# Down projection of a gated feed-forward block in seven quarter products instead of eight

## Reference: what is computed

```python
def conv_glu_ffn(h, w_up, conv_w, w_down):
    u = causal_depthwise_conv(h @ w_up, conv_w)      # w_up 1024 x 5632, three taps
    gate, val = jnp.split(u, 2, axis=-1)
    return (jax.nn.silu(gate) * val) @ w_down        # w_down 2816 x 1024

for layer in range(DEPTH):
    ...
    x = x + rms_norm(m, mix_post_norm[layer])
    f = conv_glu_ffn(rms_norm(x, ffn_pre_norm[layer]), ffn_w_up[layer], ffn_conv_w[layer], ffn_w_down[layer])
    x = x + rms_norm(f, ffn_post_norm[layer])
```

## Time and profile before

| | us |
|---|---|
| median of 3 runs | 2688.99 |
| the profiled execution, its own time | 2685.92 |
| span of that execution (first to last instruction) | 2683.9 |
| TensorE busy (share) | 2599.2 (97%) |
| VectorE busy (share) | 1636.2 (61%) |
| ScalarE busy (share) | 1115.2 (42%) |
| GpSimd busy (share) | 1179.1 (44%) |
| mean granted TensorE clock | 0.991 |

### The profile page before, as it was taken

The page is one execution under the profiler, slowest core; times in us unless marked ns, Lnnn a source line. Parts: engine busy times, 40 slices in busy tenths (PEclk is TensorE's granted clock), DMA queues, the critical chain, the costliest instruction groups (busy, mean ns, idle before and its releaser), DMA issues. The chain is left out here.

```text
span 2683.9 us, 34327 instructions
## 1 busy us (share of the span) xinstructions
PE 2599.2 (97%) x12821; PEld 2156.9 (80%) x12821; DVE 1636.2 (61%) x1740; ACT 1115.2 (42%) x1645; POOL 1179.1 (44%) x721
## 2 busy tenths in 40 slices
PE   6999999999989999999999999999989999999998
PEld 5788888888778888888888688888878888888887
DVE  5677666676168666665455658557448666665454
ACT  6445545544443443433244334434533443433242
POOL 3444333434404778784443111111413877774442
PEclk9999999999999999999999999999999999999999
DMA  3111011111432222225554111012522222234553
GB/s 120 35 38 47 31 39 47 42 36 42 124 114 101 79 85 79 87 80 168 174 175 135 61 36 48 23 55 69 160 87 78 87 71 94 71 105 154 169 189 113
DMA packets 84541, 238.07 MB, mean 89 GB/s; under 512 B 8928, under 2 KB 22816, under 8 KB 84416
## 3 DMA queue, kind: packets, MB, share of 16 engines
q1 hardware_dynamic: 84416, 236.39, 26.6%
HBM read 189.66 MB, written 46.69 MB: 88 GB/s over the span
## 5 line engine op out<-in xcount | busy, mean ns | idle before, releaser
L391 POOL TENSOR_TENSOR f_wlo<-f_raw,f_whi 128x512 fp32r<-128x512 f32 (+1 forms) x210 | 426.5, 2032 | 499.4 <-ACT f_whi L432 499.4
L703 DVE TENSOR_TENSOR f_hlo<-f_hraw,f_hhi 128x512 fp32r<-128x512 f32 x88 | 182.1, 2075 | 200.9 <-ACT f_hhi L490 200.9
L432 ACT ACTIVATE f_whi<-f_raw 128x512 fp32r<-128x512 f32 (+1 forms) x210 | 171.9, 834 | 274.5 <-PE f_value L75 252.7
L391 POOL TENSOR_TENSOR f_wlo<-f_sums,f_whi 128x512 fp32r<-128x512 f32 x144 | 188.2, 1317 | 39.8 <-ACT f_whi L432 39.8
L432 ACT ACTIVATE f_whi<-f_sums 128x512 fp32r<-128x512 f32 x144 | 90.3, 627 | 270.7 <-POOL f_sums L397 270.7
L73 PE MATMUL f_value<-x_hi,f_whi 128*128 128x512 f32 x416 | 162.6, 391 | 1.6 <-POOL f_wlo L391 1.6
L74 PE MATMUL f_value<-x_lo,f_whi 128*128 128x512 f32 x416 | 162.6, 391 | 0.0
L75 PE MATMUL f_value<-x_hi,f_wlo 128*128 128x512 f32 x416 | 162.5, 391 | 0.0
L73 PE MATMUL f_part<-f_whi,f_hhi 128*128 128x512 f32 x352 | 137.9, 392 | 0.0
L75 PE MATMUL f_part<-f_whi,f_hlo 128*128 128x512 f32 x352 | 137.5, 391 | 0.0
L74 PE MATMUL f_part<-f_wlo,f_hhi 128*128 128x512 f32 x352 | 137.1, 389 | 0.0
(11 more groups left out here) (539 smaller groups left out, 7652.2 us busy)
## 6 DMA issues: line engine op xcount, KB each, us to landing
f_raw<-in_ffn_w_up SPq DMA_DIRECT2D x88, 512.0 KB, 3.6
f_raw<-in_ffn_w_down SPq DMA_DIRECT2D x88, 512.0 KB, 3.6
hidden<-f_hid SPq DMA_DIRECT2D x44, 512.0 KB, 2.8
f_hraw<-hidden SPq DMA_DIRECT2D x88, 256.0 KB, 3.9
g_raw_first<-in_gdn_w_in SPq DMA_DIRECT2D x16, 512.0 KB, 3.6
g_raw<-in_gdn_w_in SPq DMA_DIRECT2D x16, 512.0 KB, 4.2
f_xt<-x_mid SPq DMA_DIRECT2D x16, 512.0 KB, 4.8
l_raw_first<-in_gla_w_in SPq DMA_DIRECT2D x12, 512.0 KB, 3.6
```

Of the source, the lines that this page charges most:

```text
L391: pool.tensor_tensor(part_of(w_lo, k), source, part_of(w_hi, k).bitcast(F32), ALU.subtract) \
L432: act.activation(part_of(w_hi, k), source, ACT.Copy).then_inc(s_hi, 1)
L703: dve.tensor_tensor(h_lo[d % FFN_SLOTS][:, :], h_raw[d % HIDDEN_RAWS][:, :], plain32(h_hi[d % FFN_SLOTS][:, :]), ALU.subtract).then_inc(s_ ...
```

## The change

The down projection uses seven quarter products too. The hidden rows of pair 2k and 2k+1 and the halves of the 1024 output columns are taken as 2 by 2 blocks, so a product of 128x512 by 512 columns is needed for seven operand pairs in place of eight. There are 11 pairs k (`PAIRS`) and seven products, so 77 steps of 12 matmuls. Steps 0 to 21 are stage 0 (two products, plain rows), 22 to 43 stage 1 and 44 to 65 stage 2 (two products each, with weight sums), 66 to 76 stage 3 (the last product, tokens far).

- The sums of hidden rows (`hidden_sum`, four VectorE instructions of 128x512 for each k) are made in the up projection of the next even p, and stored to DRAM beside the rows: seven blocks of 256 KB for each k. `store_hidden` runs once for two p.
- GpSimd waits for the first k's fourth sum to be stored before it makes the first weight sums of the up projection. In the down projection it makes the low parts of the first eight steps only (`BY_POOL`); VectorE makes all the others (`down_low`), and the weight sums of stages 1 and 2 (`down_sums`: two and three instructions for each k).
- The products of stages 0 to 2 are joined on VectorE (`first_quarter`, `two_products`, `three_products`, `less_fourth`, `lead_row`, `last_row`), after ScalarE has copied the first product (`keep_products`).
- No norm runs before stage 3. The squares of `m_deviation` are written to `xn`, so it waits for the store of tile t-2; `x_deviation` writes them to the tile itself.
- Four steps are held, each of 12 matmuls, so three for each token tile and step. There are four buffers for hidden rows as loaded and four for their splits, in place of three and five.

```diff
-HIDDEN_RAWS = 3
+HIDDEN_RAWS = 4
+HIDDEN_SLOTS = 4
+PAIRS = FT // 2
+OPERANDS = 7
...
+    steps = [(stage, *step) for stage in range(3)
+             for step in ((0, 0), *(x for k in range(1, PAIRS) for x in ((0, k), (1, k - 1))), (1, PAIRS - 1))]
+    steps += [(3, 0, k) for k in range(PAIRS)]
+    STEPS = len(steps)
+    HELD = STEPS - HIDDEN_SLOTS
+    BY_POOL = 8
...
+    def tile_done(stage, second, i):
+
+        if i < NT // 2 - 1:
+            return s_part, 3 * (2 * stage + second) + i + 1
+        return s_prod, FIRST_DOWN + steps.index((stage, second, PAIRS - 1)) + 1
+
+    def h_raw(d):
+        return h_raw_in[0 if d < HIDDEN_RAWS or steps[d][0] == 3 else 1][d % HIDDEN_RAWS]
+
+    def down_source(d):
+        stage, second, k = steps[d]
+        e, o = rows_of(stage, k)
+        if stage in (1, 2):
+            return sums[:, 2 * (k % 2) + 1 - second, :]
+        if stage == 3:
+            return raw[o % FFN_RAWS][:, high_cols]
+        return raw[(o if second else e) % FFN_RAWS][:, low_cols]
+
+    def m_of(t):
+        return lead_rows[t] if t < NT // 2 else acc[t - NT // 2]
+
     block = ctx.enter_context(nc.Block())
...
+        def store_hidden(pair):
+            sp.wait_ge(s_h, 2 * pair + 2)
+            sp.dma_start(hidden[pair, 2:4].rearrange("o p t -> p o t"),
+                         hid[1][:, :].rearrange("p (o t) -> p o t", o=2)).then_inc(s_store[1], 16)
+            sp.wait_ge(s_hsum, 3 * pair + 1)
+            both = hidden_sums[min(pair, 1)]
+            sp.dma_start(hidden[pair, 4:6].rearrange("o p t -> p o t"), both).then_inc(s_sstore, 16)
+            sp.wait_ge(s_hsum, 3 * pair + 2)
+            sp.dma_start(hidden[pair, 0:2].rearrange("o p t -> p o t"),
+                         hid[0][:, :].rearrange("p (o t) -> p o t", o=2)).then_inc(s_store[0], 16)
+
+        def store_fourth(pair):
+            sp.wait_ge(s_hsum, 3 * pair + 3)
+            sp.dma_start(hidden[pair, 6], hidden_sums[min(pair, 1)][:, 0, :]).then_inc(s_fstore, 16)
 
...
             if d >= HIDDEN_RAWS:
                 sp.wait_ge(s_hlo, d - HIDDEN_RAWS + 1)
-            elif PLAIN < FT:
+                if d < 2 * HIDDEN_RAWS:
+                    sp.wait_ge(s_prod, FIRST_DOWN)
+            else:
                 sp.wait_ge(s_lo, FIRST_DOWN)
-            sp.dma_start(h_raw[d % HIDDEN_RAWS][:, :], hidden[k, :, near if d < FT else far]) \
...
+            if p and p % 2 == 0:
+                store_hidden(p // 2 - 1)
             load(2 * p + 6)
+            if p and p % 2 == 0:
+                store_fourth(p // 2 - 1)
             load(2 * p + 7)
             if p == FT - 2:
...
+            if d == HIDDEN_RAWS + 2:
+                store_hidden(PAIRS - 1)
+            if d == HIDDEN_RAWS + 6:
+                store_fourth(PAIRS - 1)
+            if 2 * FT + d + 2 < 2 * FT + 7 * PAIRS:
+                load(2 * FT + d + 2)
...
+            if d == 6 * PAIRS + HIDDEN_RAWS:
+                load_x(0)
+                load_x(1)
+        for t in range(NT):
+            if t == 1 and lead is not None:
+                sp.wait_ge(*low_done(STEPS - 1))
                 lead.load(sp)
...
+        pool.wait_ge(s_fstore, 16)
         for pair in range(PLAIN, FT):
             operands(pair)
-        for d in range(STEPS):
-            low(FIRST_DOWN + d, raw[(2 * FT + d) % FFN_RAWS][:, :])
+        for d in range(BY_POOL):
+            low(FIRST_DOWN + d, down_source(d))
         if lead is not None:
             lead.small_low(pool)
-            pool.wait_ge(s_lo, FIRST_DOWN + STEPS)
+            pool.wait_ge(*low_done(STEPS - 1))
...
+        def keep_products():
+            for i in range(NT // 2):
+                act.wait_ge(*tile_done(0, 0, i))
+                act.activation(lead_rows[i][:, low_cols], first_ps[i], ACT.Copy).then_inc(s_kept, 1)
 
         def m_deviation(t):
-            if t < NT // 2:
-                act.wait_ge(s_eva, t + 1)
-                act.wait_ge(s_evd, t + 1)
-                m = acc[t]
-            else:
-                act.wait_ge(s_m, t - NT // 2 + 1)
-                m = down_ps[t - NT // 2]
-            act.activation(squares[:, :], m[:, :], ACT.Square, accum_out=ss[:, t:t + 1])
+            act.wait_ge(s_mix, 16 + 2 * t + 2 if t < NT // 2 else 24 + t - NT // 2 + 1)
+            if t >= 2:
+                act.wait_ge(s_xout[t % 2], 16 * (t // 2))
+                if pre_gain is not None:
+                    act.wait_ge(s_xs, t - 1)
+            act.activation(xn[t % 2][:, :], m_of(t)[:, :], ACT.Square, accum_out=ss[:, t:t + 1])
...
+        for d in range(STEPS - HIDDEN_SLOTS):
+            down_high(d + 5)
+            high_hidden(d + HIDDEN_SLOTS)
+            if d + HIDDEN_SLOTS == steps.index((0, 0, PAIRS - 1)) + 3:
+                keep_products()
+            n = d + HIDDEN_SLOTS - 6 * PAIRS
+            if n == 3:
+                m_deviation(0)
+            elif n == 4:
+                m_deviation(1)
+            elif n == 6:
+                x_deviation(0)
+            elif n == 7:
+                m_deviation(2)
+            elif n == 8:
+                x_deviation(1)
+            elif n == 9:
+                x_high(0)
+        m_deviation(3)
+        x_high(1)
+        x_deviation(2)
         m_deviation(4)
         if lead is not None:
             lead.small_high(act)
+        x_high(2)
+        x_deviation(3)
+        m_deviation(5)
+        x_high(3)
+        if lead is not None:
+            act.wait_ge(*low_done(STEPS - 1))
+            lead.high(act)
         x_deviation(4)
-        x_high(0)
...
+        def hidden_sum(pair, n):
+
+            even, odd = hid[0], hid[1]
+            both = hidden_sums[min(pair, 1)]
+            dve.drain()
+            if n == 0:
+                if pair:
+                    dve.wait_ge(s_fstore, 16 * pair)
+                dve.tensor_tensor(both[:, 0, :], even[:, near], odd[:, near], ALU.add)
+            elif n == 1:
+                dve.tensor_tensor(both[:, 1, :], both[:, 0, :], even[:, far], ALU.subtract).then_inc(s_hsum, 1)
+                dve.tensor_tensor(even[:, near], even[:, far], even[:, near], ALU.subtract).then_inc(s_hsum, 1)
+            else:
+                dve.wait_ge(s_sstore, 16 * (pair + 1))
+                dve.tensor_tensor(both[:, 0, :], odd[:, far], both[:, 1, :], ALU.subtract).then_inc(s_hsum, 1)
+
+        def down_low(d):
...
+            if BY_POOL <= d < STEPS:
+                dve.wait_ge(s_hi, FIRST_DOWN + d + 1)
+                k = FIRST_DOWN + d
+                dve.tensor_tensor(part_of(w_lo, k), down_source(d), plain32(part_of(w_hi, k)), ALU.subtract) \
+                    .then_inc(s_dlo, 1)
...
+        def down_sums(d):
+
+            if d >= STEPS or steps[d][0] not in (1, 2) or steps[d][1]:
+                return
+            stage, _, k = steps[d]
+            rows = rows_of(stage, k)
+            e, o = (raw[n % FFN_RAWS] for n in rows)
+            first, second = (sums[:, 2 * (k % 2) + i, :] for i in range(2))
+            for n in rows:
+                dve.wait_ge(s_raw[n % FFN_RAWS], 16 * (n // FFN_RAWS) + 16)
+            dve.drain()
+            if stage == 1:
+                dve.tensor_tensor(first, e[:, high_cols], e[:, low_cols], ALU.subtract).then_inc(s_tsum, 1)
+                dve.drain()
+                dve.tensor_tensor(second, o[:, high_cols], first, ALU.subtract).then_inc(s_tsum, 1)
+                return
+            dve.tensor_tensor(first, o[:, high_cols], e[:, high_cols], ALU.subtract).then_inc(s_tsum, 1)
+            dve.drain()
+            dve.tensor_tensor(second, first, e[:, low_cols], ALU.add).then_inc(s_tsum, 1)
+            dve.drain()
+            dve.tensor_tensor(second, second, o[:, low_cols], ALU.subtract).then_inc(s_tsum, 1)
...
+        def first_quarter():
+            for i in range(NT // 2):
+                dve.wait_ge(s_kept, i + 1)
+                dve.wait_ge(*tile_done(0, 1, i))
+                quarter(acc[i][:, low_cols], second_ps[i], lead_rows[i][:, low_cols], ALU.add)
+
...
+        def lead_row(i):
+            dve.drain()
+            dve.wait_ge(*tile_done(2, 1, i))
+            x = lead_rows[i][:, low_cols]
+            quarter(lead_rows[i][:, high_cols], second_ps[i], acc[i][:, high_cols], ALU.add)
+            quarter(x, second_ps[i], x, ALU.add)
+
+        def last_row(i):
+            dve.drain()
+            dve.wait_ge(s_m, i + 1)
+            x = acc[i][:, high_cols]
+            quarter(x, first_ps[i], x, ALU.add)
...
+            if p == 1:
+                hidden_sum(0, 0)
+                hidden_sum(0, 1)
...
+        for d in range(6 * PAIRS):
+            if d - 1 in joins:
+                joins[d - 1]()
+            down_low(d + 4)
+            hidden_low(d + 3)
+            down_sums(d + 5)
+            if d == 1:
+                hidden_sum(PAIRS - 1, 0)
+                hidden_sum(PAIRS - 1, 1)
+            elif d == 4:
+                hidden_sum(PAIRS - 1, 2)
+        at = 6 * PAIRS + 3
```

(72 more changed lines are left out.)

321 lines of the change are left out of this document (156 added, 165 removed).

## The result

The changed kernel is slower. Four runs of it gave 2739.77 us as median (2737.35 to 2740.67), four of the kernel before on the same chip 2689.74; the ratio is 1.0186, with a 95% interval of 1.0169 to 1.0204. The forecast was 2669.5 us, so it missed by 70 us and had the wrong sign.

The account below looks back on a forecast made before the run. TensorE, busy 97% of the span, was taken to bound the kernel. Down projections -21.0 and -8.8 plus 2 x (1.5 + 3.0 + 0.7) gave -19.4 us, so 2669.5 us as median; range 2656 to 2698.

Parts of the forecast that it names:

- Up projection: Seven-product pairs: four more sums in every other pair fit VectorE's 13.7 us idle in two pairs, so cost nothing.
- My own sign of being wrong: Up projection: the prediction is wrong if seven-product pairs take over 19.1 us.
- Plain pairs: Up projection: a fourth sum ahead of the value convolution makes VectorE late; 0.7 us a layer (0 to 3).
- Start of the down projection: First steps of the down projection: waits of 2.0 and 1.0, together 3.0 us a layer (2 to 5).
- the first mechanism that I named: Down projection step 2: TensorE waits 2.0 us for `hidden_low(2)`, which stands behind `activated(21)`.
- The second mechanism: Down projection about step 7: rows and weights queue behind `store_hidden(10)`, which waits for the last sums; 1.0 us of wait.
- Stage 2: Down projection: splits wait for ScalarE's copy of summed weights, 5.6 us a k, mostly covered; 1.5 us a layer (0 to 4).
- Norms and tail: From step 66's start: 73.9 us to the mixer in the first layer, 49.0 to the end in the second.
- The slower one: Rival: VectorE and weight rows bound stages 1 and 2; at 7.4 us a k, 32 us lost, 2702; chance 0.15.
- The norm chain: Rival, behind step 66: a tile costs 1 us more or ScalarE's queue holds the last steps; 2685; chance 0.13.
- The clock: Rival, first layer's stage 3: idling TensorE runs at half clock, turns up to 5 us late; 2674; chance 0.10.
- The skill against it: `hidden_sum` in the first eight down-projection steps excludes GpSimd, costing the upper 6 us, 2 us more a layer: 2673.5.

Follow-up runs that it names:

- the exchange: Changed kernel with ScalarE's `keep_first` moved ahead of the high part of S3, the same instructions otherwise: 2687.35 us, ratio to the kernel before 0.9995.
- the new tail (last kernel): Changed kernel with `keep_first` and row splits earlier, norms interleaved behind step 66, squares of tiles 3 to 7 in `raw[0]`, last hidden sums later: 2655.29 us, ratio 0.987.
- the kernel before with four such instructions and the exchange: Kernel before plus four VectorE instructions of 128x512 per even pair on an unused tile, and `keep_first` ahead of S3's high part: 2686.87 us.

## Why the prediction was wrong, step by step

The forecast for the span was 2683.9 - 19.4 = 2664.5, and it came to 2738.6: 74.1 us. Of these the up projection is 46.8, the start of the down projections 13.4, stage 2 7.6, the part behind step 66 4.0, and unchanged code 2.8 (sum 74.6; in each layer 66 steps without a wait take 180.3 where I had 180.6, which is the 0.5 left over).

- **Up projection: the step that failed.** It is the term that I put at nothing. I wrote that four instructions more in every other pair are "less than the 13.7 idle in two pairs ... So nothing there". The 13.7 us are right, and so is my bracket of 3.1 to 8.0 us for the four (measured as growth of the ring: 23.10 - 18.28 = 4.8). But 6 of the 13.7 us are the two waits of 3.0 for `keep_first`, and 4.8 more those of 1.2 for ScalarE ahead of each convolution, two in a pair: idle time of VectorE *inside* a ring of three engines, while the ring is on ScalarE or GpSimd. The sums stand where it is on VectorE, and there an added instruction lengthens it: the first three in full, the fourth, behind the gate convolution, by the 0.34 that ScalarE's scaled value tile then waits (at 1207.95). Whether sums placed into the 3.0 us themselves, between the value convolution and the next join, would be free was not tried. What had to be compared was 18.28 + 4.8 / 2 = 20.7 with 19.15. I had also counted the distance at which TensorE returns to a bank (13.7 us) as cover. Such a cover takes up one delay, not one that grows by 3.1 us every two pairs. My own sign of being wrong, a seven-product pair over 19.1 us, came. The one exchange that opens the ring brings the term to +2.5 and +3.8, near my bounds (0 to 3).
- **Plain pairs.** Estimated 0.7 (0 to 3). In the first layer TensorE waits 2.2 us for the value convolution of the third plain pair (at 876.73): the mechanism as described, the size three times mine. GpSimd's wait for the first fourth sum lasted until 871.46. This up projection starts 3.2 us later than the one I worked from, so that is the 868 that I had, and no wait of TensorE for GpSimd follows it there.
- **Start of the down projection.** Estimated 3.0 (2 to 5), measured 11.3 and 8.1. Part came out of the ring, since VectorE enters the down projection late: the exchange gave 6.3 and 2.7 of it back. The other 5 us are the first mechanism that I named (`hidden_low(2)` behind `activated(21)`), mis-sized at 2.0: with the exchange TensorE waits 3.1 and 3.6 us there, since `hidden_low(2)` itself takes 1.75 beside GpSimd's split, and the step behind the wait takes 4.2 and 4.4 us in place of 2.73, at a lower clock. The second mechanism (the weight row behind `store_hidden(10)`) cost nothing here (steps 4 to 7 take 2.73 each), as TensorE was late already; it came only when `hidden_low(2)` was moved.
- **Stage 2.** Estimated 1.5 (0 to 4), measured 6.2 and 4.4. The cause was in the sum (0.85 for ScalarE's copy), and so was 5.6 us a k (measured 6.0 and 5.9 on average over the eleven); I then let most of it be covered by the three steps that splits are ahead. It wasn't. The loads stayed hidden as costed: 4.2 us median to landing, where I had 4.4.
- **Norms and tail.** Right, and not by luck, since the links are where I had them (a first-layer tile 6.98 us against 7.1, a wait for a store's landing in the second layer's last tiles): 76.7 and 50.2 us behind step 66 against 73.9 and 49.0, and the last add of the second layer ends 45.7 us after it against 44.6. The value of a matmul was right too: 22 steps in 60.1 us are 0.228 each, and with the waits gone and the new tail (last kernel) the down projections are 17.6 and 22.6 us shorter than before.
- **Rivals.** None had the ring. The slower one put VectorE's work at the bound in the wrong stage. The norm chain was as walked. The clock I looked for between turns only; it came in the up projection (below).
- **The skill against it.** Rows 5, and now a sum of 16 columns that lasts 1.35 us beside GpSimd's of 1.31, agree with "SBUF — State Buffer", section "Who interferes with whom", of the Trainium skill, that VectorE with two SBUF inputs and GpSimd exclude each other. The rule makes a sum dear, up to 1.8 us in place of 0.7. But the kernel before with four such instructions and the exchange has the same exclusion and loses nothing. By this rule I had put the time at 2673.5, nearly as far off.

## What to carry to other kernels

Before you put work into an engine's idle time, ask what ended that idle time, and follow it back from engine to engine. If the way leads round to the same instruction one iteration earlier without passing the bounding engine, it is a ring: its period, not the engine's busy time, is what stands against the bound, and added work that lies on its way counts in full. Then look for a link that stands in the ring only by the order of a queue, since moving that one instruction can be worth more than all the work saved. When one wait is repaired, expect the next one queued behind it to show, as the weight row did.

## What the runs showed of the hardware

Some of the waits between matmuls also cost clock. Stretch of the changed kernel from the last 0.6 us of a wait of 2.68 us on (it ends at 1206.58), then its first up projection, then that of the kernel before (us, PE busy, PEld, DVE, ACT, POOL, PEclk, DMA share, GB/s):

```profile
1206.00:1210.00 4.00, 3.42 (x10) 2.66 (x11) 2.73 (x4) 3.11 (x4) 0.34 (x1) 0.66 0.42 115
...
793.00:1259.00 466.00, 444.91 (x1908) 362.24 (x1906) 331.19 (x305) 167.94 (x233) 306.01 (x208) 0.98 0.28 95
```

```profile
790.00:1232.00 442.00, 436.39 (x1906) 358.39 (x1904) 290.52 (x270) 173.33 (x236) 298.62 (x209) 0.99 0.27 89
```

The granted clock is still 1.00 while TensorE waits (1203.90 to 1206.58). It is 0.66 in the stretch shown, a mean of time at the 1.2 GHz level (0.50) and at the full one, 2.4 GHz. Of TensorE's seven waits for VectorE in this up projection, the three longest (3.17, 2.83 and 2.68 us) have a granted clock of 0.50, 0.69 and 0.61 in the 3.4 to 4.2 us behind them, the four others (1.14 to 2.20 us) one of 1.00. The length alone does not decide: in the second layer two of the five waits of 2.67 to 2.81 us are followed by 1.00.

In the whole up projection the same matmuls are busy 8.5 us longer, for six waits on `f_gate` and one on `f_hid` of 15.5 us together. So in this stretch the waits cost about half as much again as their own length, and where two stretches differ by waits, some of the difference stands in PE's busy time, not in the waits. Behind the 8.4 us wait ahead of step 2 that step takes 5.26 us in place of 2.73, all of it at a granted clock of 0.50.
